# First quarter of tokens and weights in two halves, early sums inside the last tile, and sample rows stored last in two pieces

## What is computed

```
h = rms_norm(x, norm1);  z = h @ w_in            # 2048 x 5120
u, q, f, i, g = split(z)                         # pooling input, HGRN2 query, forget, value, gate
pool_out = pool_mix(u, ...)                      # trailing means over 2, 4, 8, 16 tokens, one small product
o = hgrn2_recurrence(...)                        # 8 heads, 128 x 128 state each; norm and gate
x = x + concat(pool_out, o) @ w_o
h2 = rms_norm(x, norm2)
x = x + (silu(h2 @ w_gate) * (h2 @ w_up)) @ w_down   # width 5632
return rms_norm(x, norm_f), pool rows, recurrent states
```

## Time and profile before

| what | value |
|---|---|
| median of 3 runs | 1423.34 us (1422.92 to 1425.15) |
| profiled execution, its own time | 1423.23 us |
| its span, first to last instruction | 1421.5 us |
| PE busy | 1400.9 us |
| DVE, ACT, POOL busy | 775.3, 573.8, 214.5 us |
| mean granted clock of TensorE | 0.995 of 2.4 GHz |

### The profile page before, as it was taken

The page is one execution under the profiler, slowest core; times in us unless marked ns, Lnnn a source line. Parts: engine busy times, 40 slices in busy tenths (PEclk is TensorE's granted clock), DMA queues, the critical chain, the costliest instruction groups (busy, mean ns, idle before and its releaser), DMA issues.

```text
span 1421.5 us, 27766 instructions
## 1 busy us (share of the span) xinstructions
PE 1400.9 (99%) x10256; PEld 1384.9 (97%) x10256; DVE 775.3 (55%) x1206; ACT 573.8 (40%) x926; POOL 214.5 (15%) x329
## 2 busy tenths in 40 slices
PE   8999999999999999999999999999999999999996
PEld 7999999999999999999999999999999999999996
DVE  5668888878555544444444444444444444444443
ACT  6545555656333433333333333333333333333343
POOL 0355555553122100000000000000000000000131
PEclk9999999999999999999999999999999999999998
DMA  8556655556555555545655555565554565555453
GB/s 253 152 135 166 170 158 149 154 148 167 148 148 148 148 148 148 148 130 144 174 143 148 148 138 143 148 167 157 144 157 120 151 175 151 151 148 138 122 142 114
DMA packets 408228, 214.65 MB, mean 151 GB/s; under 512 B 4205, under 2 KB 405821, under 8 KB 408124
## 3 DMA queue, kind: packets, MB, share of 16 engines
q1 hardware_dynamic: 388775, 202.01, 52.2%
q10 hardware_dynamic: 19413, 12.10, 3.0%
HBM read 206.20 MB, written 7.89 MB: 151 GB/s over the span
## 4 chain that ended last, share of the span: by engine, by line
PE 96%; DVE 1%; DMA 1%; ACT 0%; issue 0%; ACTq 0%; DVEq 0%
PE bank L427 30%; PE bank L429 30%; PE bank L428 30%; DMA xt<-in_x_sample 1%; PE bank L544 1%; DVE w_lo L1200 0%; PE bank L777 0%; PE bank L503 0%; PE bank L504 0%; PE bank L671 0%; PE bank L505 0%; PE bank L643 0%; PE bank L596 0%; PE bank L472 0%; PE bank L652 0%
## 5 line engine op out<-in xcount | busy, mean ns | idle before, releaser
L427 PE MATMUL bank<-a_hi,w_hi 128*128 128x320 f32 x2016 | 626.5, 311 | 0.0
L429 PE MATMUL bank<-a_hi,w_lo 128*128 128x320 f32 x2016 | 623.0, 309 | 0.0
L428 PE MATMUL bank<-a_lo,w_hi 128*128 128x320 f32 x2016 | 622.9, 309 | 0.0
L1200 DVE TENSOR_TENSOR w_lo<-w_raw,w_hi 128x1024 fp32r<-128x1024 f32 (+1 forms) x412 | 455.5, 1146 | 137.1 <-ACT w_hi L821 136.3
L821 ACT ACTIVATE w_hi<-w_raw 128x1024 fp32r<-128x1024 f32 (+1 forms) x412 | 383.6, 968 | 158.8 <-PE bank L429 142.4
L427 PEld LDWEIGHTS bank<-a_hi,w_hi 128*128 128x128 f32 x2016 | 378.6, 188 | 1.5 <-issue 0.6
L428 PEld LDWEIGHTS bank<-a_lo,w_hi 128*128 128x128 f32 x2016 | 378.6, 188 | 0.7
L429 PEld LDWEIGHTS bank<-a_hi,w_lo 128*128 128x128 f32 x2016 | 378.5, 188 | 0.0
L427 PE MATMUL bank<-h_hi,w_hi 128*128 128x320 f32 x704 | 218.5, 310 | 0.0
L429 PE MATMUL bank<-h_hi,w_lo 128*128 128x320 f32 x704 | 217.4, 309 | 0.0
L428 PE MATMUL bank<-h_lo,w_hi 128*128 128x320 f32 x704 | 217.3, 309 | 0.0
(11 more groups left out here) (252 smaller groups left out, 1193.7 us busy)
## 6 DMA issues: line engine op xcount, KB each, us to landing
w_raw<-in_w_gate SPq DMA_DIRECT2D x44, 1024.0 KB, 5.6
w_raw<-in_w_up SPq DMA_DIRECT2D x44, 1024.0 KB, 5.6
w_raw<-in_w_down SPq DMA_DIRECT2D x64, 704.0 KB, 4.8
w_raw<-in_w_in SPq DMA_DIRECT2D x38, 1024.0 KB, 5.8
w_raw<-in_w_o SPq DMA_DIRECT2D x16, 1024.0 KB, 6.1
s<-in_state_hgrn ACTq DMA_DIRECT2D x8, 512.0 KB, 4.3
out<-sn ACTq DMA_DIRECT2D x8, 512.0 KB, 5.4
xt<-in_x_prompt SPq DMA_DIRECT2D x6, 256.0 KB, 8.5
```

The costliest lines, as they stand in the source:

```text
L427: pe.matmul(out, whi[:, par_, cols], r_hi, start=(k == 0), stop=False)
L428: pe.matmul(out, whi[:, par_, cols], r_lo, start=False, stop=False)
L429: last = pe.matmul(out, wlo[:, par_, cols], r_hi, start=False, stop=(k == last_k))
L1200: dve.tensor_tensor(wlo[:, par_, cols], raw[:, par_, cols], whi[:, par_, cols].bitcast(F32), SUB)\
```

## The change

**Start.** Quarter 0 is cut in two: the chunks are k 0-1, 2-3, 4-7, 8-11, 12-15 (`CHUNKS`), for tokens and weights. SP issues group 0 of each chunk, group 1 of the last two, and all weights but chunk 1's; ACT issues norm1, group 1 of chunks 0 to 2, group 2 of all, and the weights of chunk 1 (so the 512 KB of k 4-7 go to SP's queue). Splits come behind k = 0, 2, 5 and 9 (`BEHIND`). PE runs three `keep_busy` instead of four, transposes tiles 0 and 1, and from then on puts transposes behind the matmuls: tiles 2 and 3 behind product 0, tile k + 3 behind product k. **End.** The last two units are taken out of the loop; the sum over units 0 to 14 (`early_means`) is made between the two parts of unit 15. The sample rows are scaled and stored last, in two pieces.

```
-        Y_DVE = ((0, slice(0, 512)), (0, slice(512, 1024)), (2, slice(0, D)), (1, slice(0, 1024)))
+        Y_DVE = ((0, slice(0, 512)), (0, slice(512, 1024)), (1, slice(0, 1024)), (2, slice(0, 1024)), (2, slice(1024, D)))
-        QUARTERS = ((0, 4), (4, 8), (8, 12), (12, 16))
+        CHUNKS = ((0, 2), (2, 4), (4, 8), (8, 12), (12, 16))
+        BEHIND = (0, 2, 5, 9)
...
 SP
-            for quarter in range(4):
-                load_x(sp, quarter, 0)
-                if quarter >= 2:
-                    load_x(sp, quarter, 1)
-                if quarter != 1:
-                    first_weights(sp, quarter)
+            for chunk in range(5):
+                load_x(sp, chunk, 0)
+                if chunk >= 3:
+                    load_x(sp, chunk, 1)
+                if chunk != 1:
+                    first_weights(sp, chunk)
...
 PE
-            keep_busy(4)
+            keep_busy(3)
...
-            for k in range(AHEAD):
+            for k in range(2):
                 x_transposes(k)
             for k in range(KD):
-                if k + AHEAD < KD:
-                    x_transposes(k + AHEAD)
                 pe.wait_ge(ahi_ready, k + 1)
                 pe.wait_ge(alo_ready, k + 1)
...
+                for ahead in ((2, 3) if k == 0 else (k + AHEAD,)):
+                    if ahead < KD:
+                        x_transposes(ahead)
...
-                with pe.Fori(2 if final else 1, KD // 2) as j:
+                with pe.Fori(2 if final else 1, KD // 2 - (1 if final else 0)) as j:
...
-                    pe.wait_ge(x2_acc, KD - 1)
-                    for bk in (TV, OT):
-                        pe.matmul(bk[:, 2:3], acc[:, N - P:N], meanc[:, 0:1], start=True, stop=True)
-                    column_means(TV, acc, y_early)
+                    def early_means():
+                        pe.wait_ge(x2_acc, KD - 1)
+                        for bk in (TV, OT):
+                            pe.matmul(bk[:, 2:3], acc[:, N - P:N], meanc[:, 0:1], start=True, stop=True)
+                        column_means(TV, acc, y_early)
+                    unit(nd + KD - 2, 0, h_rhs, HALF_D, between=(None, y_tiles(KD - 3, 1)))
+                    unit(nd + KD - 1, 1, h_rhs, HALF_D, between=(early_means, y_tiles(KD - 2, 0)))
...
 ACT
-            for quarter in range(4):
-                if quarter < 2:
-                    load_x(act, quarter, 1)
-                if quarter == 1:
-                    first_weights(act, 1)
-                load_x(act, quarter, 2)
+            for chunk in range(5):
+                if chunk < 3:
+                    load_x(act, chunk, 1)
+                load_x(act, chunk, 2)
+                if chunk == 1:
+                    first_weights(act, 1)
...
 ACT and DVE
-                if k % 4 == 1 and k < 12:
-                    first_piece(k // 4 + 1)
+                if k in BEHIND:
+                    first_piece(BEHIND.index(k) + 1)
```

More of the change, by code:

```diff
@@ L30 @@
 HD = D // 2
-QD = D // 4
 TP, NB, TS = 256, 8, 8
@@ L210, in hybrid_kernel @@
                              "cache_loaded", "s0_loaded"))
-        x_loaded = [[sem(f"x_loaded{quarter}{i}") for i in range(3)] for quarter in range(4)]
-        w_first = [sem(f"w_first{quarter}") for quarter in range(4)]
+        x_loaded = [[sem(f"x_loaded{chunk}{i}") for i in range(3)] for chunk in range(5)]
+        w_first = [sem(f"w_first{chunk}") for chunk in range(5)]
         first_hi, first_lo, w2_loaded, w3_loaded, x_pad = (
@@ L463, in x_transposes @@
             def x_transposes(k):
-                if k % 4 == 0:
-                    for i in range(3):
-                        pe.wait_ge(x_loaded[k // 4][i], 16)
+                for chunk in range(5):
+                    if k == CHUNKS[chunk][0]:
+                        for i in range(3):
+                            pe.wait_ge(x_loaded[chunk][i], 16)
                 b4 = (SA, SB, SC, TV)[k % 4]
@@ L497, in _ @@
                 cols = slice(k * P, (k + 1) * P)
-                if k % 4 == 0:
-                    pe.wait_ge(first_hi, k // 4 + 1)
-                    pe.wait_ge(first_lo, k // 4 + 1)
+                for chunk in range(5):
+                    if k == CHUNKS[chunk][0]:
+                        pe.wait_ge(first_hi, chunk + 1)
+                        pe.wait_ge(first_lo, chunk + 1)
                 for u in range(2):
@@ L838, in square @@
                 rows, at = (P if i < 2 else NS), 2 * i + half
-                for quarter in range(2 * half, 2 * half + 2):
-                    act.wait_ge(x_loaded[quarter][i], 16)
+                for chunk in ((0, 1, 2), (3, 4))[half]:
+                    act.wait_ge(x_loaded[chunk][i], 16)
                 after(act, ss_ready, squares[0])
@@ L844, in square, with first_piece @@
                                accum_out=stat[0:rows, at:at + 1]).then_inc(ss_ready, 1)
-            def first_piece(quarter):
-                act.wait_ge(w_first[quarter], 16)
-                act.activation(side_by_side(whi, quarter), first_raw(quarter), ACT.Copy).then_inc(first_hi, 1)
+            def first_piece(chunk):
+                act.wait_ge(w_first[chunk], 16)
+                act.activation(side_by_side(whi, chunk), first_raw(chunk), ACT.Copy).then_inc(first_hi, 1)
             first_piece(0)
```

36 lines of the change are left out of this document (18 added, 18 removed).

## The result

| | before | after |
|---|---|---|
| median of the runs | 1423.41 us (1421.62 to 1425.95, 22 runs) | 1425.83 us (1422.68 to 1427.75, 22 runs) |
| ratio | | 1.0014 [1.0008, 1.0019] |
| profiled execution, its own time | 1423.23 us | 1425.32 us |
| its span | 1421.5 us | 1423.4 us |

The changed kernel is slower by some 2 us (0.14% of 1423.41 is 2.0; the medians differ by 2.4). The forecast was 1421.0, its range ended at 1423.8, so the prediction was wrong in sign and outside its range; the size is within the 0.2% that it called no change.

What follows compares the result with a forecast made beforehand. PE was taken as the bound, busy 1400.9 of 1421.5 us, with gains only where it idles or runs at low clock. The terms -2.7 + 0.9 - 0.4 = -2.2 us gave 1421.0 us, range 1419.3 to 1423.8.

Steps and rivals of the forecast that it cites:

- part 1: Start: first quarter in halves, new load order, transposes behind products; 2.7 us gained, ends 1.0 and 3.3.
- a_hi(1) waits for the landing at 10.5: Start, ACT: second weights split precedes a_hi(1), so it waits for chunk-1 weights landing at 10.5; product 1 at 12.75.
- I weigh this at 0.3 on the mean: Start, PE: low clock after the pause costs 0.5 or 1.1 us if it falls; weighed at 0.3 on the mean.
- so I add 0.2: Middle of first stage: ACT close behind, one transpose group less of lead; 0.2 us added, stage end 30.9.
- my lag of 1.3: Loads on ACT's queue: a transfer lands some 1.3 us after the queue's total reaches it.
- ACT stands longer on the second weights: Rival, start: each microsecond of later landing is one at the end; at 12.5 total 1422.8 us; chance 0.20.
- a granted clock of 0.5 for 3 us under dense products: Start, PE: listed among the signs that would make the prediction wrong.
- The 14.8: First stage behind product 3: 13 tiles and 10 transpose groups on PE, 11.5 + 3.3 = 14.8 us.
- The first rival: Clock holds and stores flow: part 1 gives 3.2, part 3 1.2, part 2 costs 0.7; 1419.6 us; chance 0.24.
- other-side rival: Start: chunk-1 weights land as late as 13.87, stage ends at 34.3, time 1424.2, slower than before; chance 0.08.
- Part 2: Last tile: early sums in its middle put ten PE instructions before the last matmuls; cost 0.88 us, ends 0.5 and 1.2.
- Part 3: Final stores: sample rows last in two pieces; gain 0.4 us, ends -0.3 and 1.2, about 225 GB/s at the end.

Runs made afterwards that it cites:

- p1: Changed kernel with the end of the kernel before (sums and stores as before), only the start changed; 1424.68 us, ratio 1.0007 to the kernel before.
- f_fill: Changed kernel with two keep_busy matmuls in each of PE's two pauses (behind the first two transposes, behind transposes 2 and 3); 1424.05 us.
- a_behind1: Changed kernel with the split of the chunk-1 weights behind k = 1 instead of k = 0; 1424.75 us.
- m: Changed kernel with ACT's two squares of the first quarter's norm behind k = 4 and 6 instead of 8 and 11; 1424.61 us.
- bf_before_fill: Kernel before with two keep_busy matmuls behind product 0, in PE's pause; 1422.44 us, ratio 0.9990.
- p2_sums_only: Kernel before with only the early sums moved between the two parts of unit 15; 1424.90 us, ratio 1.0011.
- r_reorder_only: Kernel before with only the transposes of tile k + 3 put behind product k instead of ahead of it; 1423.60 us, ratio 1.0002.
- b1_before_fill_stores: Kernel before with two keep_busy matmuls behind product 0 and the change's new store order; 1421.77 us, ratio 0.9985.
- p3_stores_only: Kernel before with only the change's new store order; 1423.04 us, ratio 0.9994.
- b2: Changed kernel with all first weights on SP, splits behind tiles 1, 3, 5, 9, fillers in both pauses, sums back, new stores kept; 1421.06 us, ratio 0.9984.
- b3: b2 with ACT's two squares behind k = 4 and 6; 1421.68 us, ratio 0.9986.

## Why the prediction was wrong

**The steps that failed are three terms of part 1: "a_hi(1) waits for the landing at 10.5" (it landed at 11.93), "I weigh this at 0.3 on the mean" (the low clock cost 1.9 us in the profile and 2.6 in the median), and "so I add 0.2" for the middle of the stage (the way behind product 3 took 0.75 us more than the sum had with it).** Product 0 came as worked out, at 10.73 (10.65), but with some luck: in four other executions with the same loads (p1, f_fill, a_behind1, m) it came at 11.47 to 11.98, since ACT's sequencer was done at 7.95 to 8.46 and not at 7.2. Product 1 came at 14.31 and not 12.75.

The halves themselves did what they should: the first weights, issued at 1.67 in both kernels, landed after 3.6 us and not after 7.4, at 5.3. That was of no use, as ACT was ready for them at 8.62 only (the prediction says so).

*The landing.* Chunk 1 landed at 11.93 in the changed kernel, and the second split started at 12.17, 12.18, 12.25 and 13.91 in the four others with the same queues. I took the curve of ACT's queue from the trace of before, 0.63 MB by 9 us, as if it were the queue's own. In the new order the same queue had moved less:

```profile
q1 hardware_dynamic: 1246, 1.26, 52.3%
q10 hardware_dynamic: 599, 0.52, 19.5%
```

(DMA queues after, to 9 us: packets, MB, share.) The 0.66 MB were through between 9.8 us (0.65) and 10.0 (0.68), not at 9.2, and the landing came 2.1 us behind that, not 1.3. The first goes with the other queue: SP's (q1) had moved 1.26 MB by 9 us against 1.17 before, and the two together 1.78 and 1.80. The total is the same and the shares are not; what sets the shares was not tried. The second is my lag of 1.3, read from two transfers of 512 and 128 KB. The Trainium skill (DMA: Bandwidth & Descriptors, on the anatomy of a DMA) has a fixed part of about 2 us, for DMAs that GpSimd issues. The 2.1 here, on ACT's queue, are of that size; the 1.3 of the kernel before are not. The rival "ACT stands longer on the second weights" was this mechanism, with a sensitivity of a microsecond at the end for each of landing. By it 11.93 puts the stage's end at 30.9 + 1.4 = 32.3. The rows say a little less: a_lo(3) was there at 16.80, so product 3 would have come at 16.9 at a full clock, 1.0 behind the forecast's 15.9. The rest of the loss is not in it.

*The clock.* There were 6.8 us at the low clock, with 4.69 us of dense work at half speed in 14.31 to 19.00 alone. Product 3 came at 18.78 and not at 16.9: 1.9 us paid where the sum had 0.3. I had named the sign ("a granted clock of 0.5 for 3 us under dense products") and priced it at a small mean, though the trace of before showed the low clock behind two pauses, of 1.5 and 1.8 us by the earlier trace rows (the prediction has 1.7 and 2.0), and the forecast itself left one of 2.2 in place. f_fill and bf_before_fill show the clock as a cost of its own: filled pauses, a clock of 1.00, and 1.8 and 1.15 us less (the intervals of f_fill and the changed kernel just touch; the changed kernel's own runs at a mean clock of 0.997 say the same, 2.6 us less). That a pause's length alone decides it is not shown: p2_sums_only has the start of before, with an even longer pause (2.47 us ahead of 15.36), and had no low clock in its execution.

*The stall in the middle.* The step "the new order leaves it one group less of lead, so I add 0.2" had the mechanism right, as r_reorder_only shows with that order alone, and the size wrong: 0.58 at tiles 9 and 10, and 0.15 at the last two tiles and behind them. From product 3 to the stage's end it is 15.75 us at a full clock, where the sum had 14.8 + 0.2 = 15.0. The 14.8 was 0.2 short too: the old order takes 14.69 with nine groups of transposes, so 15.02 with the tenth.

Together: 30.9, 1.0 for the landing, 1.9 for the clock and 0.75 for the middle make 34.55, and 0.1 is low clock behind 18.78; the profile has 34.60. Without the low clock the end would have been near 32.7, an estimate from 16.9 and 15.75, a gain of 1.2 and not of 3.0.

The first rival (the clock holds and the stores flow) fell with the clock. The other-side rival was right in its sign, but not for its reason: in the changed kernel's profile its condition, a landing near 13.87, did not hold (11.93), and the clock made up for it. f_fill's execution met the condition (13.89): the stage's end at 34.66 against the rival's 34.3, and 1425.10 against 1424.2, at a full clock.

**Part 2** was right in mechanism, and its term mis-sized: 0.88, and measured 1.0 in p2_sums_only's profile and 1.3 by the medians. The missing piece is the restart behind the sums (0.34 for the first product instead of 0.15); the 0.16 that could be had in the tail was had.

**Part 3** was right, in direction and about in size: 0.4 forecast; 0.42 between the means of nine profiles with the new stores and five with the old ones, 0.55 and 0.67 by medians of two pairs, no gain in the profile of b1_before_fill_stores. The interval of p3_stores_only still holds no change. The last stores ran at 270 and then 178 GB/s, where some 225 was named.

**What stays open.** Why ACT's sequencer is done with its ten loads at 7.21 in one execution and at 8.46 in another (below); why the way from the stage's end to the end of the last product is 0.3 to 0.45 us longer with the new start (1373.83 to 1373.94 in p1, b2 and b3, 1373.42 to 1373.59 in before, p3, r, bf and b1), of which 0.14 lie in the first product; and how large the start's own cost at full clock is: f_fill against bf_before_fill is 1.6 us, of which the sums are 1.0 to 1.3 and the stores -0.5, so 0.8 to 1.1 for the start, most of it perhaps the 0.73 in the middle and the 0.3 to 0.45 just named; it is a difference of medians whose intervals overlap.

## What to carry to other kernels

A queue's curve of bytes over time belongs to the order of loads on all queues, so when loads are moved, work the landing out from the total of all queues, and give it some room behind its last byte (1.3 to 2.1 us here). Price a stall by the starts of the work around it and not by the idle time that a profile shows (0.58 against 0.25 here). Where the trace shows the low clock behind pauses, fill them with dummy matmuls first: here two of them won 1.15 us, where the reordering won nothing, and the runs with them lie closer together. In a start where a converting engine has weights and activations in one fixed order, a smaller first piece only passes the wait to the next piece: b2_combined gained when landing, order and clock were mended together, and any one of them alone in the changed kernel left it 0.5 to 1.2 us above the kernel before.

## What the runs showed of the hardware that was not expected

- Kernels that begin alike had the low clock in different places: 14.8 to 18.2 before, 17.2 to 20.6 in p3_stores_only, nowhere in p2_sums_only. Under dense products it costs half of its time (13 matmuls in 3.1 us before, 22 in bf_before_fill), in a pause almost nothing. The five kernels with filled pauses have runs within 0.8 to 2.0 us of each other, the seven others and the changed kernel within 2.6 to 5.1.
- The issue of a load on ACT's sequencer took between 0.5 and 1.75 us for the same line, and what it delays is all of ACT's work. The row of after (4.05, one load, 0.53) has this one for the same load in f_fill:

```profile
4.04 1.75 ACTq L341 DMA_DIRECT2D xt<-in_x_prompt  x1
```

- In the changed kernel a 256 KB load of weights took 3.6 us from issue to landing on SP's queue when it was issued at 1.67 (chunk 0). With both queues full, 512 KB issued on SP's at 3.14 (chunk 2) took 8.0, and 256 KB issued on ACT's at 3.41 (chunk 1) took 8.5.
